# Between the projections of a recurrent branch: its element-wise work put between the projection tiles in another order, and the token turns of its hats put into the first inverse

## The chip, the cores and the metric

The kernel is one program on one core of a Trainium2 chip. The metric is the device time of one execution in microseconds (us). The engines run side by side and wait for one another by semaphores: TensorE (PE in the profile) multiplies matrices from SBUF into PSUM, VectorE (DVE), ScalarE (ACT) and GpSimd (POOL) work element by element, and SyncE (SP) issues the DMA transfers. Each engine takes its own instructions strictly in the order in which they were written.

## What is computed

Two transformer blocks follow each other on a sequence of 512 tokens of width 1024. The change touches the recurrent branch (`rwkv7_time_mix`) of the second block:

```python
def rwkv7_time_mix(p, shift_mu, w0, w2, a0, a2, g2, k_k, k_a, r_k, ln_x_w, ln_x_b):
    prev = jnp.pad(p, ((0, 0), (1, 0), (0, 0)))[:, :-1]
    p = p + (prev - p) * shift_mu
    r, k, v, cw, ca, cg = jnp.split(p, splits, axis=-1)
    w_log = -jax.nn.softplus(-(w0 + jnp.tanh(cw) @ w2)) - 0.5
    decay = jnp.exp(-jnp.exp(w_log.astype(jnp.float32)))
    a = jax.nn.sigmoid(a0 + ca @ a2)
    g = jax.nn.sigmoid(cg) @ g2
    kk = heads(k * k_k)
    kk = kk / jnp.maximum(jnp.sqrt(jnp.sum(kk * kk, axis=-1, keepdims=True)), 1e-12)
    k = k * (1.0 + (a - 1.0) * k_a)
    ...
    def step(state, inp):
        r_t, w_t, k_t, v_t, aa_t, bb_t = inp
        sa = jnp.einsum('bhij,bhj->bhi', state, aa_t)
        state = (state * w_t[:, :, None, :] + sa[..., None] * bb_t[:, :, None, :]
                 + v_t[..., None] * k_t[:, :, None, :])
        y = jnp.einsum('bhij,bhj->bhi', state, r_t)
        return state, y
```

`p` is the projection of the normalized input. The kernel runs the recurrence in chunks of 128 tokens: with cumulative decays the products of a chunk become matrix products, and each chunk needs the inverse of a triangular matrix.

## The kernel before

The projection `p` of the branch has 14 tiles of 128 features by 512 tokens: receptances r are tiles 0 to 3, keys 4 to 7, values 8 to 11, tile 12 holds the two low-rank inputs (decay in partitions 0 to 63, rate a in 64 to 127), and tile 13 the gate's. A tile is 24 matmuls of 128x512 on TensorE (`split_tile`, lines 611 to 613: 8 blocks of the contraction, three products of high and low parts each). Two tiles share one weight block. Each block is rounded by ScalarE (`split2_act`, L2525) and its remainder is taken by GpSimd (`splits2_pool`, L2537); TensorE waits for that before the first tile of a pair.

The functions of the stage, each written once for each engine and run in this order:

- `band_*`: the attention branch. Tile 0 of the recurrent branch is projected inside it.
- `shift_*`: the tiles 0 to 13 in that order, through two PSUM banks. VectorE scales a tile into a padded buffer `PADR` (L2827), takes the difference to the token before (L2829) and mixes (L2831); for keys it also multiplies by `k_k` (L2834). ScalarE squares (L2792), TensorE sums the squares by heads (L2767), and logarithm and exponential give the norm (L2796, L2801). After tile 13: the low-rank products (L2779, L2783), their tanh (L2809), and VectorE's scaling (L2847, L2849).
- `tiles_*`: for each of four tiles m of 128 features, VectorE's `decays` (the cumulative sum L2917 to the key product L2929 and the bonus product L2931) and `products` (L2936 to L2944), ScalarE's exponentials (L2886 to L2888), then TensorE's bonus sums (L2862) and the turn of three tiles into token order (hats `BH`, `KH`, and the values; L2873), copied by ScalarE (L2893).
- For each half of the heads: `units_*` (chunk products L2980, L2981, masked by VectorE L3034), `inverse2_*`, `state_*`.

`inverse2_pe` begins with eight steps of rows (`inv_rows_pe`, L1060: two matmuls of 128x256, one in the last) that alternate with fifteen elimination steps on VectorE (L1205, L1208) through two banks. Then come four `keep_busy` matmuls (L597), whose result nobody reads, and the first product of the assembly (L1075).

## Time and profile before

| | us |
|---|---|
| median of 3 runs | 2902.4 (2900.73 to 2904.36) |
| the profiled execution | 2909.93 |
| its span, first to last instruction | 2908.1 |
| first tile of `shift` on TensorE to the last: 2056.8 to 2133.1 | 76.3 |
| from there to the first chunk product (2179.3) | 46.2 |
| rows of the first inverse, first matmul to the first of the assembly (2194.9 to 2209.0) | 14.1 |

The profiled execution took 7.5 us more than the median of the unprofiled runs. Times within the trace are counted from the span's start. In a row of a timeline stand start, duration, engine, line, operation, output<-input, shapes and a count; in brackets, how long the engine had been idle and what ended it. A duration is that of the instruction with its pipeline: two that follow each other overlap a little, so the step from start to start is what a chain pays. An fp32 matmul leaves two records.

### The profile page before, as it was taken

The page shows a single profiled execution, that of the slowest core. Times are in us where ns is not written, and L with a number is a line of the kernel's source. Part 1 is how long each engine was busy: PE and PEld are TensorE (multiplying, and loading weights), DVE is VectorE, ACT ScalarE, POOL GpSimd, SP SyncE. Part 2 cuts the span into 40 slices and gives each one's busy share as a digit, 9 for nine tenths or more (in the row PEclk, how much of TensorE's full clock was granted, in tenths as well). Part 3 has the DMA queues.
Part 4 walks back from the last instruction along what each step waited for, and adds up shares of the span by engine and source line. Part 5 has one row for each costly group of instructions (what it writes and reads, how often), then busy time and mean ns, then how long its engine had stood idle before and what let it go on. Part 6 is the DMA issues. An engine that isn't in the chain of part 4 may idle for free.

```text
span 2908.1 us, 34074 instructions
## 1 busy us (share of the span) xinstructions
PE 2643.7 (91%) x14331; PEld 1725.7 (59%) x14331; DVE 1001.1 (34%) x1728; ACT 713.2 (25%) x1200; POOL 606.6 (21%) x185
## 2 busy tenths in 40 slices
PE   8999979879999998889888988898968899999998
PEld 7766767676658542333323323365757766788886
DVE  3267756753112311111011010134664522361331
ACT  3257633523112110010000100034231121321212
POOL 3301644623113000000000000041301122344442
PEclk9999969979999999999999999998978999999999
DMA  4302113104225799999999999951200033332231
GB/s 161 117 16 76 64 37 116 59 2 145 87 87 204 295 405 428 428 428 429 428 428 428 429 428 428 428 174 66 66 1 1 16 116 94 123 94 101 87 101 73
DMA packets 131044, 559.36 MB, mean 192 GB/s; under 512 B 7320, under 2 KB 88672, under 8 KB 103272
## 3 DMA queue, kind: packets, MB, share of 16 engines
q1 hardware_dynamic: 130056, 551.28, 48.1%
q0 software_dynamic: 864, 6.29, 0.6%
q8 instruction: 94, 1.54, 0.2%
q14 instruction: 30, 0.25, 0.0%
HBM read 547.01 MB, written 10.54 MB: 192 GB/s over the span
## 4 chain that ended last, share of the span: by engine, by line
PE 72%; DMA 13%; DVE 9%; ACT 4%; issue 2%; POOL 0%; DVEq 0%; SPq 0%; ACTq 0%; POOLq 0%
DMA S<-in_w_up 11%; PE PS L611 8%; PE PS L613 8%; PE PS L612 8%; PE PS L2215 7%; PE PS L2182 7%; PE PS L601 4%; PE PS L2165 2%; PE PS L3407 2%; PE PS L3409 2%; PE PS L3410 2%; PE PS L3245 2%; PE PS L2226 1%; DMA S<-in_w_down 1%; DVE PS L1205 1%
## 5 line engine op out<-in xcount | busy, mean ns | idle before, releaser
L2182 PE MATMUL PS<-S 128*64 128x512 f32 x2048 | 457.0, 596 | 72.2 <-DMA S<-in_w_up 68.0
L611 PE MATMUL PS<-r_block,r_block 128*128 128x512 f32 x1040 | 417.8, 402 | 4.2 <-POOL r_block L2537 2.3
L613 PE MATMUL PS<-r_block,r_block 128*128 128x512 f32 x1040 | 405.5, 390 | 0.0
L612 PE MATMUL PS<-r_block,r_block 128*128 128x512 f32 x1040 | 405.1, 390 | 0.0
L2537 POOL TENSOR_TENSOR r_block<-S,r_block 128x2048 fp32r<-128x2048 f32 x57 | 268.1, 4704 | 478.4 <-ACT r_block L2525 469.6
L2182 PEld LDWEIGHTS PS<-S 128*64 128x64 f32 x2048 | 140.9, 137 | 379.0 <-issue 247.4
L491 POOL TENSOR_TENSOR r_block<-S,r_block 128x2048 fp32r<-128x2048 f32 x40 | 183.3, 4582 | 551.7 <-ACT r_block L483 330.0
L2215 PE MATMUL PS<-S 128*64 128x512 f32 x1024 | 225.6, 597 | 6.6 <-DMA S<-in_w_down 3.3
L611 PEld LDWEIGHTS PS<-r_block,r_block 128*128 128x128 f32 x1040 | 195.5, 188 | 50.9 <-issue 9.0
L612 PEld LDWEIGHTS PS<-r_block,r_block 128*128 128x128 f32 x1040 | 195.6, 188 | 44.9 <-issue 5.8
L613 PEld LDWEIGHTS PS<-r_block,r_block 128*128 128x128 f32 x1040 | 195.3, 188 | 41.1
L2411 POOL TENSOR_TENSOR S<-S 128x1024 f32<-128x1024 f32 x4 | 9.5, 2407 | 976.9 <-DVE S L2399 976.9
L2525 ACT ACTIVATE r_block<-S 128x2048 fp32r<-128x2048 f32 x57 | 109.2, 1918 | 367.3 <-PE PS L613 196.2
L2374 DVE SCALAR_TENSOR_TENSOR S<-S,PS 128x512 f32<-128x512 f32 x32 | 22.0, 688 | 487.0 <-ACT S L2302 463.6
L2215 PEld LDWEIGHTS PS<-S 128*64 128x64 f32 x1024 | 75.8, 138 | 145.4 <-issue 140.6
L601 PE MATMUL PS<-S 128*128 128x512 f32 x256 | 110.5, 592 | 0.0
L2381 DVE TENSOR_TENSOR S<-S,PS 128x512 f32<-128x512 f32 x32 | 20.6, 684 | 256.4 <-PE PS L2182 256.4
L3407 PE MATMUL PS<-r_block,r_block 128*128 128x512 f32 x256 | 99.8, 390 | 1.6 <-DVE S L3457 1.6
L483 ACT ACTIVATE r_block<-S 128x2048 fp32r<-128x2048 f32 x40 | 76.4, 1909 | 99.2 <-DMA S<-in_w_in 68.4
L3409 PE MATMUL PS<-r_block,r_block 128*128 128x512 f32 x256 | 99.7, 389 | 0.0
L3410 PE MATMUL PS<-r_block,r_block 128*128 128x512 f32 x256 | 99.6, 389 | 0.0
L601 PEld LDWEIGHTS PS<-S 128*128 128x128 f32 x256 | 48.6, 190 | 59.6 <-issue 59.3
(487 smaller groups left out, 3768.7 us busy)
## 6 DMA issues: line engine op xcount, KB each, us to landing
S<-in_w_gate SPq DMA_DIRECT2D x64, 2048.0 KB, 17.9
S<-in_w_up SPq DMA_DIRECT2D x64, 2048.0 KB, 21.0
S<-in_w_down SPq DMA_DIRECT2D x64, 2048.0 KB, 25.6
S<-in_w_in SPq DMA_DIRECT2D x57, 1024.0 KB, 5.3
S<-in_w_up SPq DMA_DIRECT2D x16, 1024.0 KB, 5.5
S<-in_w_down SPq DMA_DIRECT2D x16, 1024.0 KB, 4.8
S<-decay_rows SPq DMA_DIRECT2D x8, 1024.0 KB, 7.0
S<-in_w_out SPq DMA_DIRECT2D x8, 1024.0 KB, 5.0
```

The lines of the kernel that those rows point to most:

```text
L491: pool.tensor_tensor(r32(w), w, rounded(WH[k % 2]), ALU.subtract).then_inc(sem("w_low"), 1)
L601: mm = pe.matmul(out, w[:, dc, off:off + P], src[:, dc, :], start=(dc == 0), stop=(dc == DC - 1))
L611: pe.matmul(out, wh, r32(HT[:, dc, :]), start=(dc == 0), stop=False)
L612: pe.matmul(out, wh, r32(low[:, dc, :]), start=False, stop=False)
L613: mm = pe.matmul(out, wl, r32(HT[:, dc, :]), start=False, stop=(dc == DC - 1))
L2182: mm = pe.matmul(PS[c * CAP:(c + 1) * CAP, 2 + 2 * m + g, :], XE[:, 2 * q + r, e * CAP:(e + 1) * CAP], w[:, r, 1024 * g + 512 * c:1024 * g ...
L2215: mm = pe.matmul(PS[c * CAP:(c + 1) * CAP, 6 + half, :], HE[e][:, f, :], w[:, f % 4, 512 * half:512 * half + 512], start=(f == 0), stop=(f ...
L2525: act.activation(r32(WH[k % 2]), slot2(name), ACT.Copy).then_inc(sem("w2_high"), 1)
L2537: pool.tensor_tensor(r32(w), w, rounded(WH[k % 2]), ALU.subtract).then_inc(sem("w2_low"), 1)
L3407: pe.matmul(PS[:, n, :], uh, r32(grid(wh.rearrange("p a b -> p (a b)"), 2)[:, f % 2, s]), start=first, stop=False)
L3409: pe.matmul(PS[:, n, :], uh, r32(wl[:, f % 2, s]), start=False, stop=False)
L3410: mm = pe.matmul(PS[:, n, :], ul, r32(grid(wh.rearrange("p a b -> p (a b)"), 2)[:, f % 2, s]), start=False, stop=last)
```

## The change

- The tiles come in the order 12, 13, keys 4 to 7, receptances 0 to 3, values 8 to 11 (`R_ORDER`), through four PSUM banks; i counts the place in that order below, t the tile.
- The shift is computed in another way: VectorE scales the tile into its frame, ScalarE writes mu times the tokens before into the tile's PSUM bank (511 columns), VectorE multiplies the frame's first column by 1-mu and then computes (1-mu) times the frame plus the bank.
- Low-rank products stand behind places 2 and 3, their tanh at 3 and 4, `decays` behind the scaling of places 3 to 6, head sums at place 6, norms at 7 to 9, `products` (with the bonus product) behind the scaling of places 9 to 12. Keys times `k_k`, and the square, are now computed by ScalarE. Norm logarithms and exponentials are computed in PSUM.
- The values are turned into token order behind places 12 and 13. The eight turns of the hats and the four bonus sums stand between the row steps of the first inverse, their copies on ScalarE after the inverse's corners, and TensorE waits for the last of them ahead of the `keep_busy`.
- `tiles_*` is gone. Low-rank weights load ahead of the branch's second weight block, the gate's weights ahead of the merge's first, and the third weight buffer of the branch lies in another place. LOW3, NORMF and SIG have other addresses.

The core of the diff (left out are addresses, semaphore tables, and removed lines that stand in the listing above):

```diff
+        R_ORDER = (12, 13, 4, 5, 6, 7, 0, 1, 2, 3, 8, 9, 10, 11)
...
+            load2(("r", j), cols2(a["w_in_2"], B2_R + P * R_ORDER[2 * j]), full, "r_proj", 2 * (j + 1))
...
+            third = B2 + 16384 if n < where2[("r", 0)] else M_X if n < where2[("m", 0, 0)] else B2 + 22528
...
+        KKN = [BH[:, m, :] for m in range(4)]
+        KSQ = [at(B2 + 15360 + 1024 * m, T) for m in range(4)]
+        CS = [TM[:, m, :] for m in range(4)]
+        KP = [TM[:, 4 + m, :] for m in range(4)]
...
+        def turn_pe(pe, n, src):
+            if n >= 2:
+                pe.wait_ge(*count("t_tok", n - 1))
+            for tc in range(TC):
+                mm = pe.transpose(PS[:, 6 + n % 2, block_of(tc)], src[:, block_of(tc)], ident)
+            mm.then_inc(sem("t_turned"), 1)
...
+        def hat_turn_pe(pe, j):
+            m, w = divmod(j, 2)
+            turn_pe(pe, 4 + j, (BH, KH)[w][:, m, :])
+
+        def tokens_act(act, n):
+            dst, m = (VT, n) if n < 4 else ((BT, KTK)[n % 2], (n - 4) // 2)
+            act.wait_ge(*count("t_turned", n + 1))
+            act.activation(dst[:, :, block_of(m)], grid(PS[:, 6 + n % 2, :], TC), ACT.Copy).then_inc(sem("t_tok"), 1)
+
...
+            def low_rank(m):
+                if m >= 2:
+                    pe.wait_ge(*count("r_gates", 2 * m - 3))
+                pe.matmul(PS[:, 4 + m % 2, :], W2[0:64, block_of(m)], FR[0:64, 12, :], start=True, stop=True)\
+                    .then_inc(sem("r_low"), 1)
+                if m >= 2:
+                    pe.wait_ge(*count("r_gates", 2 * m - 2))
+                pe.matmul(PS[:, 6 + m % 2, :], A2[64:128, block_of(m)], FR[64:128, 12, :], start=True, stop=True)\
+                    .then_inc(sem("r_low"), 1)
+
+            for i in range(1, 14):
+                if i % 2 == 0:
+                    await_split2(pe, ("r", i // 2))
+                if i >= 4:
+                    pe.wait_ge(*count("r_shift", i - 3))
+                split_tile(pe, PS[:, i % 4, :], parts2(("r", i // 2)), P * (i % 2), LOW3).then_inc(sem("r_proj"), 1)
+                if i == 2:
+                    pe.wait_ge(*count("lora_in", 32))
+                    pe.wait_ge(*count("r_lora", 1))
+                    low_rank(0)
+                    low_rank(1)
+                if i == 3:
+                    low_rank(2)
+                    low_rank(3)
+                if i == 6:
+                    pe.wait_ge(*count("r_gates", 8))
                     for m in range(4):
                         pe.wait_ge(*count("t_sq", m + 1))
                         pe.matmul(PS[:, 4 + m, :], const("heads2"), KSQ[m], start=True, stop=True).then_inc(sem("t_sum"), 1)
...
+                if i == 12:
+                    pe.wait_ge(*count("t_norm", 4))
+                    value_turn_pe(pe, 0)
+            for m in range(1, 4):
+                value_turn_pe(pe, m)
...
         def shift_act(act):
...
+            def gates(m):
+                for w, (dst, bias) in enumerate(((LW, s_w0h), (AG, s_a0h))):
+                    act.wait_ge(*count("r_low", 2 * m + w + 1))
+                    act.activation(dst[:, m, :], PS[:, 4 + 2 * w + m % 2, :], ACT.Tanh, bias=bias[:, m:m + 1], scale=0.5)\
+                        .then_inc(sem("r_gates"), 1)
+
+            def key_squares(m):
+                act.wait_ge(*count("r_shift", 3 + m))
+                act.activation(KKN[m], FR[:, 4 + m, :], ACT.Copy, scale=vec("k_k", m)).then_inc(sem("t_kk"), 1)
+                act.activation(KSQ[m], FR[:, 4 + m, :], ACT.Square, scale=vec("k_k", m)).then_inc(sem("t_sq"), 1)
+
+            def exps(m):
+                act.wait_ge(*count("t_cs", 2 * (m + 1)))
+                act.activation(KH[:, m, :], CS[m], ACT.Exp, scale=-1.0).then_inc(sem("t_exps"), 1)
+                act.activation(LW[:, m, :], LW[:, m, :], ACT.Exp).then_inc(sem("t_exps"), 1)
+
+            for i in range(14):
+                t = R_ORDER[i]
+                if i % 2 == 0 and i < 12:
+                    split2_act(act, ("r", i // 2 + 1))
+                act.wait_ge(*count("r_copied", i + 1))
+                act.activation(PS[:, i % 4, 1:T], frame(t)[:, 0:T - 1], ACT.Copy, scale=vec("mu", t)).then_inc(sem("r_prev"), 1)
+                if i == 1:
+                    act.wait_ge(*count("r_shift", 1))
+                    act.activation(FR[0:64, 12, :], FR[0:64, 12, :], ACT.Tanh).then_inc(sem("r_lora"), 1)
+                if i == 2:
+                    act.wait_ge(*count("r_shift", 2))
+                    act.activation(SIG, SIG, ACT.Tanh, scale=0.5).then_inc(sem("r_lora"), 1)
+                    act.wait_ge(*count("r_halves", 5))
+                if i == 3:
+                    gates(0)
+                    gates(1)
+                if i == 4:
+                    gates(2)
+                    gates(3)
+                if 3 <= i < 7:
+                    key_squares(i - 3)
+                if 5 <= i < 9:
+                    exps(i - 5)
+                if i == 8:
                     for m in range(4):
                         act.wait_ge(*count("t_max", m + 1))
...
+                        act.activation(PS[:, 4 + m, :], PS[:, 4 + m, :], ACT.Ln, scale=2.0 ** 30).then_inc(sem("t_ln"), 1)
                     for m in range(4):
                         act.wait_ge(*count("t_ln", m + 1))
...
+                        act.activation(PS[:, 4 + m, :], PS[:, 4 + m, :], ACT.Exp, scale=-0.5, bias=s_c30).then_inc(sem("t_rn"), 1)
+                    for m in range(4):
+                        act.activation(AR[m][:, :, 1, :], grid(CS[m], TC), ACT.Exp).then_inc(sem("t_exps"), 1)
+                if i == 9:
+                    act.wait_ge(*count("t_ends", 12))
+                    act.activation(e_mid, cmid, ACT.Exp).then_inc(sem("t_ends_exp"), 1)
+                    act.activation(e_end, cend, ACT.Exp).then_inc(sem("t_ends_exp"), 1)
+                    act.activation(e_rest, e_rest, ACT.Exp).then_inc(sem("t_ends_exp"), 1)
+                if i == 13:
+                    tokens_act(act, 0)
+            for n in range(1, 4):
+                tokens_act(act, n)
...
+            def decays(m):
+                C = CS[m]
+                Cg = grid(C, TC)
+                dve.wait_ge(*count("r_gates", 2 * m + 1))
...
+                dve.wait_ge(*count("r_gates", 2 * m + 2))
...
+                dve.wait_ge(*count("r_sig", 2 * m + 1))
...
+            def faded_keys(m):
+                dve.wait_ge(*count("r_sig", 2 * m + 2))
+                dve.tensor_scalar(KP[m], AG[:, m, :], vec("k_a", m), s_ka1[:, m:m + 1], ALU.mult, ALU.add).then_inc(sem("t_kp"), 1)
...
+                dve.tensor_tensor(KP[m], KP[m], FR[:, 4 + m, :], ALU.mult).then_inc(sem("t_kp"), 1)
...
+                dve.wait_ge(*count("t_norm", m + 1))
...
+                dve.tensor_tensor(KH[:, m, :], KP[m], KH[:, m, :], ALU.mult).then_inc(sem("t_hats"), 1)
+                dve.wait_ge(*count("t_exps", 8 + m + 1))
+                dve.wait_ge(*count("r_shift", 7 + m))
+                dve.tensor_tensor(AR[m][:, :, 1, :], AR[m][:, :, 1, :], grid(r, TC), ALU.mult).then_inc(sem("t_ar"), 1)
+                dve.wait_ge(*count("t_hats", 2 * m + 2))
+                dve.scalar_tensor_tensor(KP[m], r, vec("r_k", m), KP[m], ALU.mult, ALU.mult).then_inc(sem("t_bonus"), 1)
...
+            dve.tensor_scalar(s_mu1, vec("mu", 0, 14), -1.0, 1.0, ALU.mult, ALU.add).then_inc(sem("r_halves"), 1)
...
+            for i in range(14):
+                t = R_ORDER[i]
+                f = frame(t)
+                dve.wait_ge(*count("r_proj", i + 1))
+                dve.tensor_tensor(f, PS[:, i % 4, :], RSB, ALU.mult).then_inc(sem("r_copied"), 1)
+                if 3 <= i < 7:
+                    decays(i - 3)
+                if i == 7:
+                    for m in range(4):
+                        dve.wait_ge(*count("t_sum", m + 1))
+                        dve.tensor_scalar(PS[:, 4 + m, :], PS[:, 4 + m, :], 1e-24, None, ALU.max).then_inc(sem("t_max"), 1)
+                    faded_keys(0)
+                if i == 8:
+                    faded_keys(1)
+                    faded_keys(2)
+                    faded_keys(3)
+                if i == 9:
+                    for m in range(4):
+                        dve.wait_ge(*count("t_rn", m + 1))
+                        dve.tensor_tensor(KKN[m], KKN[m], PS[:, 4 + m, :], ALU.mult).then_inc(sem("t_norm"), 1)
+                if 9 <= i < 13:
+                    products(i - 9)
+                dve.wait_ge(*count("r_prev", i + 1))
+                dve.tensor_scalar(f[:, 0:1], f[:, 0:1], s_mu1[:, t:t + 1], None, ALU.mult)
+                dve.scalar_tensor_tensor(f[:, 1:T], f[:, 1:T], s_mu1[:, t:t + 1], PS[:, i % 4, 1:T], ALU.mult, ALU.add)\
+                    .then_inc(sem("r_shift"), 1)
+                if i == 6:
+                    dve.wait_ge(*count("r_lora", 2))
+                    dve.tensor_scalar(SIG, SIG, 0.5, 0.5, ALU.mult, ALU.add).then_inc(sem("r_sig"), 1)
 
...
-                pe.wait_ge(*count("t_tok", 12))
+                pe.wait_ge(*count("r_shift", 14))
+                pe.wait_ge(*count("t_ar", 8))
...
             for p in range(8):
                 inv_rows_pe(pe, w, n, sel, p)
+                if hf == 0:
+                    hat_turn_pe(pe, p)
+                    if p % 2:
+                        bonus_pe(pe, p // 2)
+            if hf == 0:
+                pe.wait_ge(*count("t_tok", 12))
...
+            if hf == 0:
+                for j in range(4, 12):
+                    tokens_act(act, j)
...
+            if hf == 0:
+                dve.wait_ge(*count("t_bonus_sum", 4))
+                dve.tensor_copy(bon, grid(PS[:, 5, 0:TC * H2], TC)).then_inc(sem("t_bon"), 1)
...
-                dve.wait_ge(*count("t_tok", 12))
+                dve.wait_ge(*count("t_tok", 4))
...
-                pool.wait_ge(*count("t_bon", 1))
-                pool.wait_ge(*count("t_tok", 12))
+                pool.wait_ge(*count("t_ar", 8))
+                pool.wait_ge(*count("t_bonus", 4))
...
+            pe.wait_ge(*count("t_bon", 1))
...
-                if n == where2[("r", 6)]:
-                    sp.wait_ge(*count("b_yat", 4))
+                if n == where2[("r", 1)]:
                     sp.dma_start(W2[0:64, :], a["w2_2"][0]).then_inc(sem("lora_in"), 16)
                     sp.dma_start(A2[64:128, :], a["a2_2"][0]).then_inc(sem("lora_in"), 16)
+                if n == where2[("r", 2)]:
+                    sp.wait_ge(*count("x2_kept", 16))
+                if n == where2[("m", 0, 0)]:
+                    sp.wait_ge(*count("r_proj", 14))
+                    sp.wait_ge(*count("low2_out", 32))
                     sp.dma_start(G2, a["g2_2"][0]).then_inc(sem("g2_in"), 16)
-                if n == where2[("m", 0, 0)]:
                     sp.wait_ge(*count("s_y", TC))
```

**Order, TensorE in the first inverse.** Before, the chunk products (L2981) are followed by all fifteen row matmuls, the `keep_busy` and the assembly:

```order
L2981 MATMUL PS<-S 128x256
L1060 MATMUL PS<-S 128x256 x15
L597 MATMUL PS<-S 128x256 x4
L1075 MATMUL PS<-S 64x32 x32
L597 MATMUL PS<-S 128x256
```

Now (line numbers are one higher; L2996 is the chunk product, L2770 a turn's four transposes, L2788 a bonus sum's four matmuls):

```order
L2996 MATMUL PS<-S 128x256
L1061 MATMUL PS<-S 128x256 x2
L2770 MATMUL PS<-S 128x128 x4
L1061 MATMUL PS<-S 128x256 x2
L2770 MATMUL PS<-S 128x128 x4
L2788 MATMUL PS<-S 128x2 x4
L1061 MATMUL PS<-S 128x256 x2
L2770 MATMUL PS<-S 128x128 x4
L1061 MATMUL PS<-S 128x256 x2
```

A turn, and behind every second one a bonus sum, now stands between any two row steps; four such pairs of turns in all.

**Order, VectorE at the last tiles of the projection.** Before, three instructions a tile:

```order
L2827 TENSOR_TENSOR S<-PS,S 128x512
L2829 TENSOR_TENSOR S<-S 128x512
L2831 SCALAR_TENSOR_TENSOR S<-S 128x512
L2841 TENSOR_TENSOR S<-S 128x512 x4
L2843 TENSOR_SCALAR S<-S 128x512
L2847 TENSOR_SCALAR S<-S 128x512
```

Now, one place (`products`, first column, mix; then the scaling of the next tile, L2943):

```order
L2962 TENSOR_SCALAR S<-S 128x1
L2963 SCALAR_TENSOR_TENSOR S<-S,PS 128x511
L2943 TENSOR_TENSOR S<-PS,S 128x512
L2916 TENSOR_TENSOR S<-S 128x4x128
L2919 TENSOR_TENSOR S<-S 128x512
L2921 TENSOR_TENSOR S<-S 128x512
L2923 TENSOR_TENSOR S<-S 128x512
L2926 TENSOR_TENSOR S<-S 128x4x128
L2928 SCALAR_TENSOR_TENSOR S<-S 128x512
L2962 TENSOR_SCALAR S<-S 128x1
L2963 SCALAR_TENSOR_TENSOR S<-S,PS 128x511
L2943 TENSOR_TENSOR S<-PS,S 128x512
```

Six instructions of `products` moved between the scaling of a tile and its mix, at four places.

**Order, ScalarE at place 8.** Before, the logarithms and the exponentials of the norm with the block splits between them and the tail's tanh behind:

```order
L2792 ACTIVATE S<-S 128x512 x2
L2525 ACTIVATE r_block_581<-S 128x2048
L2796 ACT_TABLE_LOAD
L2796 ACTIVATE S<-S 128x512 x4
L2801 ACT_TABLE_LOAD
L2801 ACTIVATE S<-S 128x512 x4
L2803 ACTIVATE S<-S 64x512
L2804 ACTIVATE S<-S 128x512
L2809 ACTIVATE S<-PS,S 128x512 x8
```

Now (L2527 is the split of a weight block, L2850 the tokens before, L2842 and L2843 exponentials of the decays, L2871 and L2874 the norms, L2876 the exponentials for `AR`):

```order
L2527 ACTIVATE r_block_643<-S 128x2048
L2850 ACTIVATE PS<-S 128x511
L2842 ACTIVATE S<-S 128x512
L2843 ACTIVATE S<-S 128x512
L2871 ACT_TABLE_LOAD
L2871 ACTIVATE PS<-PS 128x512 x4
L2874 ACT_TABLE_LOAD
L2874 ACTIVATE PS<-PS,S 128x512 x4
L2876 ACTIVATE S<-S 128x4x128 x4
L2850 ACTIVATE PS<-S 128x511
L2879 ACTIVATE S<-S 128x16
```

Twelve activations and both table loads stand in one row there, behind the split of one block and ahead of the next place's tokens and the next split.

## Rows read from the trace of the kernel before

**Rows 1.** Chain that ended last, from the last projection tile: start, us, what

```profile
2132.89 0.24 PE PS L613
...
2144.26 1.22 DVE S L2917
...
2175.39 0.70 DVE S L2944
...
2179.32 0.71 PE PS L2980 x4
```

**Rows 2.** Windows: stretch, length, busy (count) of PE, PEld, DVE, ACT, POOL, PEclk, DMA share, GB/s

```profile
2056.80:2133.00 76.20, 74.73 (x322) 59.91 (x320) 49.94 (x54) 21.84 (x21) 28.19 (x6) 1.00 0.20 62
2133.00:2179.30 46.30, 23.80 (x97) 17.47 (x97) 39.03 (x73) 19.58 (x36) 0.00 (x0) 0.67 0.00 0
...
2194.90:2201.00 6.10, 6.07 (x14) 4.54 (x15) 3.54 (x10) 0.00 (x0) 0.00 (x0) 0.50 0.01 3
2201.00:2206.10 5.10, 4.55 (x17) 2.73 (x16) 4.30 (x16) 0.00 (x0) 0.00 (x0) 0.99 0.01 2
```

**Rows 3.** VectorE's groups by line and shape, 2133 to 2180: busy us, mean ns

```profile
L2917 DVE TENSOR_TENSOR_SCAN S<-S 128x512 f32<-128x512 f32 x4 | 4.9, 1223 | 0.3
...
L2942 DVE TENSOR_TENSOR S<-S 128x512 f32<-128x512 f32 x4 | 2.8, 692 | 0.1
...
L2918 DVE TENSOR_SCALAR S<-S 128x512 f32<-128x512 f32 x4 | 2.1, 523 | 0.0
L2847 DVE TENSOR_SCALAR S<-S 128x512 f32<-128x512 f32 x4 | 1.7, 427 | 3.1 <-ACT S L2809 3.1
```

**Rows 4.** Timeline of ScalarE: a block split, a table load, four logarithms

```profile
2107.98 1.92 ACT L2525 ACTIVATE r_block<-S 128x2048 fp32r<-128x2048 f32 x1 [3.31 <-PE PS L613]
2109.91 1.28 ACT L2796 ACT_TABLE_LOAD   x1
2116.54 2.42 ACT L2796 ACTIVATE S<-S 128x512 f32<-128x512 f32 x4 [5.34 <-DVE S L2838]
```

**Rows 5.** Timelines of GpSimd and VectorE at three places, side by side

```profile
2088.21 4.63 POOL L2537 TENSOR_TENSOR r_block<-S,r_block 128x2048 fp32r<-128x2048 f32 x1 [6.26 <-ACT r_block L2525]
...
2088.40 4.72 DVE L2834 TENSOR_SCALAR S<-S 128x512 f32<-128x512 f32 x1
...
141.87 4.63 POOL L491 TENSOR_TENSOR r_block<-S,r_block 128x2048 fp32r<-128x2048 f32 x1 [6.79 <-ACT r_block L483]
...
145.56 0.95 DVE L907 TENSOR_TENSOR S<-S 128x1 f32<-128x1 f32 x1 [21.60 <-ACT S L786]
...
288.07 4.61 POOL L491 TENSOR_TENSOR r_block<-S,r_block 128x2048 fp32r<-128x2048 f32 x1 [7.82 <-ACT r_block L483]
...
288.92 0.68 DVE L1379 SCALAR_TENSOR_TENSOR S<-S,PS 128x512 f32<-128x512 f32 x1
```

**Rows 6.** Timeline of TensorE: head sums, and low-rank products behind an idle stretch

```profile
2113.16 3.59 PE L2767 MATMUL PS<-S 128*128 128x512 f32 x8
...
2136.17 1.10 PE L2779 MATMUL PS<-S 64*128 64x512 f32 x1 [3.05 <-ACT S L2803]
...
2140.09 0.59 PE L2779 MATMUL PS<-S 64*128 64x512 f32 x1
```

**Rows 7.** Timeline of TensorE in `tiles`: bonus sums and turns

```profile
2149.06 1.83 PE L2862 MATMUL PS<-S 128*128 128x2 f32 x8 [6.76 <-DVE S L2931]
...
2161.67 1.02 PE L2862 MATMUL PS<-S 128*128 128x2 f32 x8 [1.96 <-DVE S L2931]
...
2172.88 2.92 PE L2873 MATMUL PS<-S 128*128 128x128 f32 x12 [1.33 <-DVE S L2944]
...
2177.94 0.66 PE L2873 MATMUL PS<-S 128*128 128x128 f32 x4 [0.20 <-ACT S L2893]
```

**Rows 8.** Timeline of TensorE in the first inverse, from its first row matmul

```profile
2194.93 7.85 PE L1060 MATMUL PS<-S 128*128 128x256 f32 x20 [5.92 <-DVE S L1193]
...
2206.12 1.89 PE L597 MATMUL PS<-S 128*128 128x256 f32 x8
2208.99 1.20 PE L1075 MATMUL PS<-S 64*64 64x32 f32 x35 [0.98 <-DVE S L1218]
```

182 lines of the change are left out of this document (24 added, 158 removed), and 6 rows, old and new, of the table CHAINS.

## The prediction

> **What bounds the kernel now.** I read first the chain that ended last, around the recurrent branch [rows 1]. TensorE's last projection tile ends at 2133.1, VectorE's serial chain follows (it starts `decays` at 2144.26, ends `products` at 2175.39), and the next large TensorE work begins at 2179.32. Then the windows [rows 2]: up to 2133 TensorE is busy 74.73 of 76.20 us; in the 46.30 us behind, VectorE is busy 39.03 and TensorE 23.80, much of that at the half clock (0.67 on average). So this stage has two halves with different limits, and the second is all dependency: nothing of the merge or of the chunk products may start. In the first half VectorE is busy 49.94, but this contains waits inside instructions [rows 5]: GpSimd's split ran from 2088.21 for 4.63, and a VectorE instruction that began at 2088.40, and that takes 0.42 to 0.52 elsewhere [rows 3], took 4.72. An instruction with one operand in PSUM took its normal 0.68 beside such a split, at 288.92. The reader is to see that VectorE's room between tiles is less than its idle time.
>
> **The shift stage, up to tile place 6.** One tile costs TensorE (74.73 busy, less 3.4 of head sums) / 13 = 5.5 [rows 2]; I use 5.45. Place 1 starts at 2056.8 and place 2 ends at 2069.5, with the same wait for GpSimd's first split as before (1.5). New on TensorE behind it: four low-rank pairs. At the full clock a record takes 0.59 with its pipeline [rows 6], a step some 0.1 less; the two products of a pair run beside each other, two steps a pair, so 1.9 for the first two pairs. Place 3 ends at 2076.8. The third pair waits for a gate: VectorE's scaling 0.7, ScalarE's tokens before 0.6, one tanh 0.6: 2.0 idle. With the last two pairs place 4 starts at 2081.0, and three tiles end at 2097.3. Up to here TensorE pays 3.9 for the low-rank products and 2.2 for waits. Head sums cost 3.4 as before [rows 6], and 0.4 for the last square, since ScalarE does three 0.6 activations behind the scaling of place 6.
>
> **From there VectorE is the bound.** Terms from start to start: an fp32 SBUF instruction of 512 columns 0.62, or 0.72 where the next needs its result (0.69 in the row), a one-source one 0.35 to 0.5, a scan 1.2, a small copy about 0.1 [rows 3]. `decays` with its two scalings is 3.7, a faded key 1.2, `products` with the bonus 4.0, scaling plus first column plus mix 0.7 + 0.1 + 0.7 = 1.5. At place 5 VectorE comes late: ScalarE gets its tokens at 2093.4, does 2.2 of squares and exponentials, splits block 4 for 1.9 [rows 4], and GpSimd holds 2098.1 to 2102.7. VectorE's fourth `decays` waits that long. From 2102.7:
>
> - rest of place 6: 3.7 + 0.8 + 0.4 = 4.9, to 2107.6
> - place 7: 1.5, four maxima 2.5, one faded key 1.2 = 5.2, to 2112.8
> - place 8: 1.5, three faded keys 3.5, wait for GpSimd (split 5 runs to 2116.5) 3.1 = 8.1, to 2120.9
> - place 9: 1.5, four norms 2.5, `products` 4.0 = 8.0, to 2128.9
> - place 10: 1.5, `products` 4.0, wait for split 6 (to 2132.6) 3.1 = 8.6, to 2137.5
> - places 11 and 12: 5.5 each, to 2148.5
> - place 13: scaling 0.7, ScalarE 0.7, mix 0.8 = 2.2, to 2150.7
>
> TensorE for comparison: place 7 starts at 2101.1, place 11 ends at 2128.3. Place 12 needs split 6, and ScalarE is in its long row at place 8 from 2113.4: tokens 0.6, two exponentials 1.1, load 1.3, four logarithms 2.4, load 1.3, four exponentials 2.6, four more 2.4, then tokens and three small ones 1.0, to 2126.0 [rows 4]; then the split, 1.9, and GpSimd, 4.6: 2132.6. TensorE idles 4.3. Behind 3.05 idle its clock had fallen, and a low-rank record took 1.10 instead of 0.59 [rows 6]; I charge 1.7. Place 13 ends at 2146.0, 4.7 ahead of VectorE. So these waits on TensorE cost nothing beyond VectorE's sum; cut them and VectorE is still last. Two value turns with their copies remain, some 2.5 (0.97 each at the half clock, 2.92 / 3 [rows 7]): the chunk products start at 2153.5 instead of 2179.3. That is **25.8 us earlier**.
>
> **What is moved and costs nothing there.** SyncE's low-rank loads move ahead of the second block's; the new wait for `x2_kept` holds the third block's load, which the stage needs only 5 tiles later; the gate's weights are needed in the second half of the heads. ScalarE's extra 14 token writes (0.6 each, 8.4) fill idle time except the 0.7 at place 13. Any of them would cost its duration if TensorE were waiting for it. The mask's wait (`t_tok` 4), and GpSimd's select (1.9, now ahead of place 13's end) stay under the ten microseconds of chunk products.
>
> **The first inverse.** Here TensorE gets eight turns and four bonus sums. Before, its 30 row records plus gaps took 11.2 (2194.93 to 2206.1), led by VectorE's elimination, then `keep_busy` and assembly at 2208.99: 14.1 in all [rows 8]. The clock was half to about 2201 and full then [rows 2]; 14 records in 6.1 us give 0.42 to 0.44 each at half, and some 0.24 at full. At half clock: rows 1.7, turn 0.97, rows 1.7, turn 0.97, bonus 1.83 [rows 7] = 7.2. Then full: 22 row records 5.2, five turns 0.66 each 3.3, two bonus sums 1.02 each 2.0 = 10.5. Rows end after 17.7 instead of 11.2. Then the last turn and bonus 1.7 and `keep_busy` 1.9 [rows 8]: assembly after 21.3 instead of 14.1, **7.2 us more**. What covered them before is gone: TensorE, not VectorE, is now last at each row step. ScalarE's eight copies (0.6 each) follow each turn and are ready before the next but one. Bounds: all at full clock, rows end after 7.1 + 4.6 + 3.1 = 14.8 and the cost is 4.3; all at half, 30 x 0.43 + 7 x 0.97 + 3 x 1.83 = 25.2 and then 6.6, so 17.7. I take the value in between since the idle 5.92 ahead and the work that raised the clock are the same [rows 8].
>
> **Sum.** -25.8 + 7.2 = -18.6 us in the span of 2908.1. All behind the stage waits on it, so it shifts whole. The profiled execution lies 7.5 above the median of 2902.4; the difference carries over: **2883.8 us**.
>
> **A rule weighed.** Two things speak of the shared SBUF access. In [rows 5] a VectorE instruction of a single column with two SBUF inputs that began at 145.56 took 0.95, to the end of GpSimd's 4.63. No row shows a one-column instruction with one SBUF source beside a split. The Trainium skill, "SBUF — State Buffer", section "Who interferes with whom", says that copies and `tensor_scalar` can enter a two-port mode and then contend with GpSimd, the later one blocked for the whole of the earlier. By it the 14 new first-column instructions wait for a split too. Put into the walk above, the end moves by 0.2 us, since VectorE is blocked there by its large instructions anyway; without it the sum stands. By the same section whoever starts first holds the pair for a whole instruction, which is the third rival's mechanism in its weakest form.
>
> **Rivals.**
> - *Turns hidden, VectorE less blocked.* Were no wait for GpSimd paid, VectorE would end 3 to 4 earlier, where TensorE's own sum stands; with the turns at full clock, 4.3. Change -26 to -23: 2876 to 2880. For it: clock was up at 2201 with gaps in the work. Against: [rows 5]. Chance 0.15.
> - *Longer cross-engine chains.* Every hand-over between VectorE, ScalarE and TensorE costs some 0.05 in my walk; at 0.2, the end moves by 1.7; two more full locks of 4.6, or the half clock through the inverse (10.5 more), give -13 to -3: 2889 to 2899. Chance 0.22.
> - *Starved splits (slower).* VectorE issues strings of 4 us of SBUF instructions. If a string kept GpSimd out until its end ([rows 5] shows only VectorE as the one blocked), the six splits would start up to 4 later each, and TensorE's stall for each, with the clock lost (4 + 1.7) x 6 = 34, would exceed the 25.8 saved: with the 7.2, +15, 2918. It decides from about 3.1 us a split. Against: each place has two or three instructions with a PSUM operand that leave a gap. Chance 0.03.
> - *It doesn't do what it says*: if place 13's chain waited for something long on ScalarE, the tail of 46 would come back. The order shows nothing behind it. 0.01, within 0.2%.
>
> **How the numbers follow.** Forecast -23 to -13, 2879 to 2890: 0.59. With the two neighbours the range 2876 to 2892 holds some 8 in 10. A measurement of this kernel can tell about 0.2% (5.8 us) from no change: faster by more 0.92 (the forecast, the first rival and most of the second), within 0.05, slower 0.03.
>
> **What would show it.** In the profile after: first chunk product near 2153 and last projection tile near 2146; six GpSimd splits of 4.6 with VectorE instructions as long beside them; an idle stretch of 3 to 5 us on TensorE before place 12, released by GpSimd; from the first row matmul to the assembly 21 us instead of 14. Wrong would be: TensorE waiting for `r_shift` at earlier places (VectorE's terms too small), or a first inverse that has not grown.

## The result, and the profile after

The changed kernel took 2878.8 us (median of 4 runs, 2873.91 to 2883.0) and the kernel before 2901.68 (4 runs): ratio 0.9923, 95% interval 0.9906 to 0.994. That is 22.9 us less, where the forecast said 18.6. The profiled execution after took 2878.79 us, its span was 2877.0.

The two profiled spans differ by 31.1 us, more than the medians. Comparing when the same VectorE instruction starts in both traces shows which part is the change's. These are rows of the timeline of VectorE, first the last bias addition of the banded attention, which no edit touches, before and after; then the last group of the whole kernel, before and after:

```profile
2041.56 0.69 DVE L2725 SCALAR_TENSOR_TENSOR S<-PS,S 128x512 f32<-128x512 f32 x1 [1.05 <-PE PS L2630]
```

```profile
2032.97 0.69 DVE L2727 SCALAR_TENSOR_TENSOR S<-PS,S 128x512 f32<-128x512 f32 x1
```

```profile
2899.87 4.87 DVE L3359 SCALAR_TENSOR_TENSOR S<-S 128x1024 f32<-128x1024 f32 x4 [0.80 <-ACT S L3353]
```

```profile
2868.74 4.87 DVE L3387 SCALAR_TENSOR_TENSOR S<-S 128x1024 f32<-128x1024 f32 x4 [0.80 <-ACT S L3381]
```

So 8.6 us of the 31.1 had arisen in unchanged code ahead of the stage (the profiled execution before was 8.3 above the median of its four runs), and 22.5 are the change's. All stretches below are therefore distances between two instructions of one trace, not absolute times.

The chain that ended last, after, answers to [rows 1]: VectorE's last scaling, mix and the value turns now lead straight into the chunk products (L2995), at 2145.13 in the chain, where [rows 1] had 2179.32; the corners, the row matmuls (L1061), and between them turns and bonus sums (L2788), lead to the assembly (L1076):

```profile
2141.20 0.61 DVE S L2943
2141.84 0.69 ACT PS L2850
...
2143.19 1.94 PE PS L2770 x8
2145.13 1.16 PE PS L2995 x4
...
2146.90 9.67 DVE S L3061 x16
...
2161.13 2.05 PE PS L1061 x4
2163.18 0.85 PE PS L2770 x4
...
2168.92 0.87 PE PS L1061 x4
2169.78 0.44 PE PS L2770 x4
2170.22 0.79 PE PS L2788 x8
...
2177.57 1.89 PE PS L598 x8
2179.47 2.01 PE PS L1076 x64
```

The windows of after, with the columns of [rows 2]: the tiles; the 4.4 us before the value turns; turns, products and corners; the first inverse in two pieces; what follows it:

```profile
2047.90:2138.80 90.90, 84.17 (x349) 64.12 (x348) 66.24 (x115) 44.73 (x63) 27.60 (x6) 0.96 0.15 47
2138.80:2143.20 4.40, 0.56 (x6) 0.35 (x4) 3.64 (x8) 1.36 (x3) 1.89 (x1) 0.96 0.22 60
2143.20:2161.10 17.90, 12.15 (x72) 10.20 (x72) 10.51 (x19) 5.31 (x11) 4.46 (x1) 0.88 0.00 1
2161.10:2167.40 6.30, 6.27 (x25) 5.37 (x25) 3.08 (x8) 1.20 (x2) 0.04 (x1) 0.55 0.00 0
2167.40:2179.40 12.00, 12.00 (x80) 10.65 (x80) 7.20 (x25) 3.58 (x6) 1.80 (x1) 1.00 0.01 2
2179.40:2200.60 21.20, 19.98 (x447) 17.15 (x447) 6.70 (x12) 7.49 (x13) 0.95 (x1) 1.00 0.01 2
```

[Rows 2] had a second half of 46.3 us, in which VectorE was busy 39.03 and TensorE half of the time at a clock of 0.67. That half is gone: VectorE's work lies within the tiles, where it is now busy 66.24 of 90.9 us, and the clock there is 0.96.

From VectorE's first scaling (2058.88 before, 2049.60 after) to the first mask it is 121.68 us before and 97.30 after, -24.4. From the first row matmul to the assembly it is 14.06 before [rows 8] and 18.27 after, +4.2. Ahead of the first scaling 0.7 go, and behind the assembly another 1.5: the granted clock was 0.84 before in the 21 us behind it, and 1.00 after, and the first 25 us there are 2.0 shorter. Together -22.5, with 0.1 between mask and rows. This is that window of before:

```profile
2209.00:2230.00 21.00, 20.60 (x423) 17.10 (x424) 6.51 (x11) 7.04 (x12) 1.12 (x2) 0.84 0.01 2
```

### The profile page after: what moved, and what is told of

Its sections match the earlier page's. It is cut to its first block, busy times and chain, and to the rows that moved or that the text cites. A ratio compares the mean times of both kernels' runs of the same rounds, so it can differ in the third digit from the quotient of the medians.

```text
span 2877.0 us, 34074 instructions
## 1 busy us (share of the span) xinstructions
PE 2626.2 (91%) x14331; PEld 1711.4 (59%) x14331; DVE 982.3 (34%) x1724; ACT 723.9 (25%) x1218; POOL 605.7 (21%) x185
## 4 chain that ended last, share of the span: by engine, by line
PE 71%; DMA 13%; DVE 9%; ACT 4%; issue 2%; POOL 1%; DVEq 0%; SPq 0%; ACTq 0%; POOLq 0%
DMA S<-in_w_up 11%; PE PS L612 8%; PE PS L614 8%; PE PS L613 8%; PE PS L2216 7%; PE PS L2183 7%; PE PS L602 4%; PE PS L2166 2%; PE PS L3435 2%; PE PS L3437 2%; PE PS L3438 2%; PE PS L3273 2%; PE PS L2227 1%; DMA S<-in_w_down 1%; PE PS L633 1%
## 5 line engine op out<-in xcount | busy, mean ns | idle before, releaser
L2539 POOL TENSOR_TENSOR r_block<-S,r_block 128x2048 fp32r<-128x2048 f32 x55 | 257.9, 4690 | 484.5 <-ACT r_block L2527 475.8
L492 POOL TENSOR_TENSOR r_block<-S,r_block 128x2048 fp32r<-128x2048 f32 x40 | 183.3, 4582 | 551.0 <-ACT r_block L484 329.4
L612 PEld LDWEIGHTS PS<-r_block,r_block 128*128 128x128 f32 x1040 | 195.8, 188 | 56.3 <-issue 10.9
L2527 ACT ACTIVATE r_block<-S 128x2048 fp32r<-128x2048 f32 x57 | 109.2, 1918 | 337.6 <-PE PS L614 166.7
```

Of the source, the lines that this page charges most:

```text
L492: pool.tensor_tensor(r32(w), w, rounded(WH[k % 2]), ALU.subtract).then_inc(sem("w_low"), 1)
L612: pe.matmul(out, wh, r32(HT[:, dc, :]), start=(dc == 0), stop=False)
L2527: act.activation(r32(WH[k % 2]), slot2(name), ACT.Copy).then_inc(sem("w2_high"), 1)
L2539: pool.tensor_tensor(r32(w), w, rounded(WH[k % 2]), ALU.subtract).then_inc(sem("w2_low"), 1)
```

## The experiments

Whole times of one kernel scatter by 10 to 20 us, stretches of equal code by 0.1 where the clock is the same. So the table gives both. Every kernel is the changed one with one edit, unless said otherwise. P0, P4 and P9 are VectorE's scalings of places 0, 4 and 9, M the first mask, R the first row matmul, A the assembly; P0-M is the time from P0 to M, and so on; us. The ratio is that of runs taken together on one chip; the medians of different chips are compared with less confidence.

| kernel | P0-M | P4-M | P9-P10 | M-R | R-A | median | ratio to before, 95% |
|---|---|---|---|---|---|---|---|
| changed | 97.3 | 66.1 | 7.8 | 14.2 | 18.3 | 2878.8 | 0.9923 (0.9906 to 0.994) |
| changed, again | 97.3 | 65.7 | 7.8 | 14.5 | 17.4 | 2880.2 | 0.9927 (0.9909 to 0.9946) |
| turns_ahead | 109.8 | 79.8 | 7.8 | 14.8 | 14.1 | 2885.9 | 0.9956 (0.9935 to 0.9978) |
| turns_units | 97.5 | 66.2 | 7.8 | 18.3 | 14.1 | 2880.9 | 0.9946 (0.9925 to 0.9966) |
| turns_idle | 98.3 | 65.1 | 7.8 | 14.2 | 14.1 | 2875.0 | 0.9889 (0.987 to 0.9907) |
| lowrank_later | 96.6 | - | 7.8 | 14.3 | 17.2 | 2879.5 | 0.9927 (0.9904 to 0.995) |
| short_splits | 94.8 | 63.2 | 9.7 | 14.2 | 17.1 | 2875.1 | 0.9911 (0.9879 to 0.9943) |
| products_last | 108.2 | 78.2 | 5.4 | 14.3 | 17.2 | 2887.4 | 0.9938 (0.9918 to 0.9959) |
| split6_early | 99.1 | 67.8 | 12.1 | 14.4 | 17.3 | 2881.0 | 0.9915 (0.9898 to 0.9931) |
| no_max | 97.7 | 66.4 | 7.8 | 14.2 | 18.3 | 2876.4 | 0.9909 (0.9886 to 0.9933) |
| split6_ln | 95.5 | 64.1 | 9.4 | 14.6 | 14.1 | 2872.7 | 0.9908 (0.9884 to 0.9931) |
| rebalanced | 95.6 | - | 13.3 | 14.2 | 14.1 | 2869.4 | 0.9899 (0.9879 to 0.9918) |
| rebalanced2 | 95.2 | - | 11.4 | 14.2 | 14.1 | 2874.2 | 0.9909 (0.9894 to 0.9924) |

The step from place 3 to place 4, with the low-rank pairs, took 10.7 to 13.9 us in the ten kernels that have the same code there, depending on TensorE's clock behind its wait of 2.17 us. These are its windows (length, TensorE busy, clock, DMA) from the first of these products on, in the changed kernel and in products_last, where the clock stayed up behind the same wait:

```profile
2071.03:2075.03 4.00, 4.00 (x9) 0.57 0.64 224
```

```profile
2074.91:2078.91 4.00, 4.00 (x13) 1.00 0.65 225
```

In turns_idle it came back only within place 4. That is why P4-M stands beside P0-M. The changed kernel run again confirms the result:

> The changed kernel once more, unaltered, on the same chip as the two others, as the yardstick for both: 0.992 of the kernel before; its stretches as in its first profile: place 4 scaling to first mask 66.1, first mask to first row matmul 14.2, first row matmul to assembly 17 to 18.3. If the 22.9 us of the first comparison were partly chance, the ratio would come out above 0.994.

### Where the turns cost least

**turns_ahead.**

```diff
 # shift_pe, behind the value turns
+... (waits for the hats and the bonus products)
+for p in range(8):
+    hat_turn_pe(pe, p)
+    if p % 2: bonus_pe(pe, p // 2)
 # inverse2_pe
-if hf == 0:
-    hat_turn_pe(pe, p)
-    if p % 2: bonus_pe(pe, p // 2)
 # ScalarE's eight copies move with them (left out)
```

> The changed kernel with its eight hat turns and four bonus sums taken out of the first inverse and put on TensorE right behind the value turns, ahead of the chunk products. My theory (in the inverse they cost 4.2 us, since TensorE then is last at each row step; ahead of the products nothing hides them but 1 us or so): the stretch from the first row matmul to the assembly falls back from 18.3 to about 14, and the first mask comes 6 to 8 us later (eight turns of 0.66 and four bonus sums of 0.8 at the full clock, 8.5, of which the first turns may begin while TensorE idles before 2143), so 2 to 4 us slower than the changed kernel: about 2881 to 2883. Rival 1 (the turns in the inverse cost nothing themselves, the 4.2 us there are the half clock that any stretch behind an idle one has): the inverse stays at 17 to 18, and the kernel is 6 to 8 us slower, 2886. Rival 2 (what costs in the inverse is the whole 8.5): the time stays, 2879.

The inverse fell to 14.1, as before the change, but the first mask came 12.5 us later, not 6 to 8. TensorE's timeline:

```profile
2140.05 3.80 PE L2770 MATMUL PS<-S 128*128 128x128 f32 x16 [3.93 <-ACT S L2784]
2143.64 1.70 PE L2788 MATMUL PS<-S 128*128 128x2 f32 x8
2145.21 1.95 PE L2770 MATMUL PS<-S 128*128 128x128 f32 x8
2146.95 1.71 PE L2788 MATMUL PS<-S 128*128 128x2 f32 x8
```

Behind the 3.93 idle a pair of turns took 1.74 from start to start and a bonus sum 1.56 (2145.21 to 2146.95 to 2148.51), twice the 0.88 and 0.79 that they take in the changed kernel's chain: all 15 us up to the chunk products passed at a granted clock of 0.50. From place 4 the mask is 13.7 later. My theory was right on where they cost more and had the size too small, by the clock; the time came out at rival 1's 2886, whose mechanism the inverse of 14.1 refutes. Against the plain place ahead of the products, hat turns and bonus sums in the inverse saved 13.7 + 0.6 - 4.2, some 10 us by the stretches and 7 by the medians.

**turns_units** puts a hat turn behind every second chunk product and the bonus sums behind them all.

```diff
 # units_pe, in the loop over the 16 products
+if n in (3, 5, 7, 8, 9, 11, 13, 15):
+    hat_turn_pe(pe, ...)
 # behind the products of m == 1
+for k in range(4): bonus_pe(pe, k)
 # left out: a wait for the bonus products; the turns leave the inverse,
 # and ScalarE's copies stand ahead of its corners
```

> The changed kernel with its eight hat turns put between the chunk products of the first half (one after every second product) and the four bonus sums behind the products, ahead of the first row matmul, where TensorE waited 5.8 us. My theory (turns cost only where TensorE is last; between the products VectorE's 16 masks of 0.61 set the pace and TensorE is busy 8.35 of 14 us): first mask and first row matmul stay within 1 us of their distance from the stage's start, the stretch from first row matmul to assembly falls from 18.3 to 14 or below, since TensorE is busy right before it and its clock is up: 4 to 6 us faster than the changed kernel, 2873 to 2875. Rival 1 (the half clock comes whatever TensorE did before): the inverse falls to 14 only, 2875. Rival 2 (the turns wait for ScalarE's copies and delay the chunk products and so the masks by 4 us or more): no gain, 2879.

Rival 2 held in size, not in cause. The inverse lost its 4.2, and M-R grew by 4.1. ScalarE's copies did not set the pace: the last ended at 2158.84, and ScalarE's first corner began at 2158.97, 0.12 behind VectorE's copy L1189, as in the changed kernel (0.11). Two chunk products with a turn need 1.65 of TensorE at the full clock where two masks need 1.29 of VectorE, which now waited for TensorE:

```profile
2152.57 0.66 PE L2770 MATMUL PS<-S 128*128 128x128 f32 x4
2153.16 0.71 PE L2995 MATMUL PS<-S 64*128 64x256 f32 x4
2153.70 0.60 PE L2996 MATMUL PS<-S 64*128 64x256 f32 x4
2154.23 0.66 PE L2770 MATMUL PS<-S 128*128 128x128 f32 x4
...
2158.04 3.63 PE L2788 MATMUL PS<-S 128*128 128x2 f32 x32
2163.50 2.04 PE L1061 MATMUL PS<-S 128*128 128x256 f32 x4 [1.83 <-DVE S L1194]
```

```profile
2155.98 1.29 DVE L3063 TENSOR_TENSOR S<-PS,S 128x512 f32<-128x512 f32 x2 [0.37 <-PE PS L2996]
```

The four bonus sums, 3.63, lay in an idle stretch and cost nothing. And even with TensorE at work until 2161.7 the first rows ran at half the clock (2.04 for four records, 2.05 in the changed kernel), but the inverse came to the same 14.1 as before the change.

**turns_idle** uses what the two had shown.

```diff
 # shift_pe, behind tile place 13
+value_turn_pe(pe, 1)
+for j in range(5): hat_turn_pe(pe, j)
 # shift_act, ahead of the write for place 13
+for n in range(5): tokens_act(act, n)
 # inverse2_pe: the four bonus sums ahead of the rows;
 # only hat turns 5 to 7 stay, behind row pairs 4 to 6
 # left out: waits, and the order of the copies
```

> The changed kernel with five hat turns put behind tile place 13, where TensorE idled 3.84 us (2139.3 to 2143.2) until ScalarE had copied the first value turn (that copy now comes ahead of ScalarE's write for place 13), the four bonus sums behind the chunk products, where TensorE idled 5.8 us (in the run with the turns between the products they took 3.63 there and delayed nothing), and three hat turns left in the last rows of the inverse. My theory (an instruction of TensorE costs nothing only where TensorE idles in the present order, and eight turns between the products cost 3.9 since there VectorE waited for TensorE at every second mask): place 0 scaling to first mask stays at 97 to 98 us, first mask to first row matmul at 14.2, first row matmul to assembly falls from 18.3 to 14 to 15.5. Sum 3 to 4 us less than the changed kernel, 2875. Rival 1 (what the turns cost follows them wherever they stand: 12.5 ahead, 3.9 between the products, 4.2 in the inverse): no gain. Rival 2 (ScalarE, whose five copies now precede its write for place 13, delays the last mix by their 3.3): the first mask 2 to 3 us later, gain 1.

As the theory had it: P4-M 65.1 (1.1 less), M-R 14.2, R-A 14.1, in all 5.3 less than the changed kernel; the medians, from two comparisons, say 3.8, and the two ratios, 0.9889 and 0.9923, have intervals that just touch, so that the gain rests on the stretches. Rival 1 falls: what a turn costs depends on the place.

### Who is last in the tiles

**lowrank_later** (`if i == 3` to `if i == 4` ahead of `low_rank(2)`, `low_rank(3)`).

> The changed kernel with the last two of the four low-rank pairs behind tile place 4 in place of 3. In the changed kernel TensorE waits 2.17 us for a tanh gate there, and its eight products then run at the half clock for 3.95 us. My theory: at place 4 the gates are long done, no wait and no half clock, so place 4 starts about 6 us earlier and place 5 about 4 us earlier (two pairs at the full clock take about 2); VectorE, which from place 6 on has no idle time, starts its gapless stretch 4 us earlier, and the chunk products start 3 to 4 us earlier: 2875. Rival 1 (the stage is bound later by GpSimd's split 6 and the ScalarE row before it, which follow VectorE's places): the same 3 to 4 us. Rival 2 (VectorE is the bound over the whole stage from place 3, so that an earlier tile 4 changes nothing): first mask as in the changed kernel, 2879. Rival 3 (GpSimd's locks fall on other instructions and give the gain back): 0 to 1 us.

Rival 3. Place 4 came 5.2 us earlier as expected (26.0 instead of 31.2 behind P0), but only 0.7 of it reached the first mask. At place 6 TensorE waited 2.3 for ScalarE's square, which now stood behind a block split, and VectorE was caught by GpSimd more fully:

```profile
2093.73 4.73 POOL L2539 TENSOR_TENSOR r_block<-S,r_block 128x2048 fp32r<-128x2048 f32 x1 [9.76 <-ACT r_block L2527]
```

```profile
2093.99 4.75 DVE L2895 TENSOR_SCALAR S<-S 128x512 f32<-128x512 f32 x1
```

**short_splits** (GpSimd's remainder of blocks 4, 5 and 6 replaced by a memset of the same tile).

```diff
+if name in (("r", 4), ("r", 5), ("r", 6)):
+    pool.memset(rounded(w), 0.0)
+    continue
 pool.tensor_tensor(r32(w), w, rounded(WH[k % 2]), ALU.subtract)
```

> The changed kernel with GpSimd's remainder of the recurrent blocks 4, 5 and 6 left out: a memset of the same tile stands in its place, so the low weight part of six tiles is zero and the output loses precision there. In the changed kernel the three remainders took 4.6 us each and three VectorE instructions beside them took 4.39, 3.23 and 3.65 in place of 0.43, 0.54 and 0.69, 9.6 us more; TensorE waited 2.9 us for the last. A memset of this size on GpSimd took 1.80, and VectorE instructions with SBUF operands beside it were not longer (0.76, 0.71). My theory (VectorE is the bound from place 6 on, its lost time counts until TensorE's own sum takes over: tile place 13 would end 2.9 + 1.7 earlier, and VectorE's scaling, mix and the value turns follow it): first mask 5 to 7 us earlier than in the changed kernel, 2872 to 2874. Rival 1 (TensorE and not VectorE is the bound): only the 2.9 us wait and its clock go, 3 to 4.6 us. Rival 2 (full slope, VectorE alone): 9.6 us, 2869. Rival 3 (the long instructions are no loss, the waits only moved): 0.

It gave 2.9 us (P4-M), less than my theory, near the lower end of rival 1. These are VectorE's waits in it:

```profile
DVE S L2946 <- PE PS L614: 4.1, 4, 2.8
DVE S L2961 <- ACT PS L2877: 1.7, 1, 1.7
```

Of the first lock, of 3.9 us, nothing was to be had: place 7 came 9.36 behind place 6 in both kernels, since TensorE needs that long for head sums and tile. Of the second 2.2 came off the step from place 8 to 9 (7.62 to 5.43, which is TensorE's tile), and 1.8 went back into the next step, where VectorE waited for ScalarE's exponentials. Only the third came off whole, 8.40 to 5.42. So the prediction's statement that VectorE is the bound from place 6 on, with all its locks on the path, falls: three engines lie within 3 us of each other.

**no_max** takes 2.5 us of work off VectorE at place 7 (`bias=s_tiny` in the logarithm, no `ALU.max`).

> The changed kernel without VectorE's four maxima of 2.48 us in all at tile place 7: the lower bound of the head sums is added inside ScalarE's logarithm instead, which no longer waits for VectorE. Theory after the short splits (taking 9.6 us of locks off VectorE moved the first mask by only 2.5 us, since VectorE then waited 2.8 for TensorE's place 7 and 1.7 for ScalarE's norms row): VectorE, TensorE and ScalarE's row lie within 3 us of each other at places 7 to 9, so 2.5 us off VectorE alone gives 1.5 to 2.5, and ScalarE's row starts 1 to 2 us earlier, which takes its wait away too: first mask 1.5 to 2.5 us earlier, 2877. Rival 1 (slope one, VectorE alone is the bound): 2.5, and with the earlier row more is to be had in the short splits only. Rival 2 (TensorE sets the pace at places 7 to 9): 0 to 0.5.

Rival 2: P4-M 66.4, no gain at all, although the median happens to be 2.4 lower. Place 7 was TensorE's (5.44 from scaling to scaling, 0.39 of it idle on VectorE), and place 8 began when it did before.

**products_last** moves the four `products(m)` behind the loop over the places.

> The changed kernel with the four calls of the products taken out from between tile places 9 to 12 and put behind the mix of place 13, so that only the decays, maxima, faded keys and norms are left between the tiles. Theory (in the changed kernel VectorE sets the pace at these places, but TensorE is close below it: its own place 13 ended at 2138.7 with 2.9 of waiting, VectorE's last scaling began at 2141.1): the last scaling moves 1 to 2.5 us ahead, and 24 instructions of 0.69 or 16.3 us stand behind the mix, with the value turns beside them: first mask 10 to 13 us later than in the changed kernel, 2889 to 2892. So about half of the 24.4 us that this stage got shorter is due to the products between the tiles. Rival (TensorE's half clock and the locks matter more than the place of VectorE's work): under 6 us, 2885.

P4-M grew by 12.1 and P0-M by 10.9, 10 to 13 expected. So putting the products between the tiles is worth about half of the 24.4 us. How the other half divides is not shown: no run moves decays, squares, maxima, keys or norms back, and the parts need not add up, since turns_ahead alone made P0-M 12.5 longer.

**split6_early.**

```diff
 # shift_act, place 8, behind the exponentials of the norms
+split2_act(act, ("r", 6))
 for m in range(4):
     act.activation(AR[m][:, :, 1, :], ..., ACT.Exp)
```

> The changed kernel with ScalarE's high part of the sixth recurrent block taken from ahead of tile place 10 and put into its long row at place 8, between the four exponentials of the norms and the four of the receptance side. GpSimd then begins the split about 3 us earlier, and TensorE's wait of 2.9 us ahead of place 12 and the half clock behind it (24 products, about 1.7) should be gone. Theory (VectorE is the last at places 9 to 13, with TensorE's place 13 ending 2.4 us before VectorE's last scaling begins): the wait goes, VectorE's lock of 3 us only moves to another instruction, and place 0 scaling to first mask stays at 97.3, 2879. Rival 1 (TensorE is the bound): 3 to 4.6 us less, 2875. Rival 2 (the exponentials behind it, 1.9 later, are then late for VectorE's products of place 9): 1 to 2 us more, 2880 to 2881.

TensorE's wait ahead of place 12 went, and P4-M grew by 1.7, which is rival 2's size but not its cause (no exponential was late). As expected the waits of TensorE there cost nothing beyond VectorE's, but the lock did not only move. It hit a string of products in full, 4.3 in place of 3.0; P9-P10 is 12.1 instead of 7.8, P10-P11 then 5.4 instead of 8.4. These are GpSimd and VectorE:

```profile
2122.07 5.02 POOL L2539 TENSOR_TENSOR r_block<-S,r_block 128x2048 fp32r<-128x2048 f32 x1 [7.92 <-ACT r_block L2527]
```

```profile
2122.65 4.99 DVE L2922 TENSOR_TENSOR S<-S 128x512 f32<-128x512 f32 x1
```

**split6_ln** is turns_idle with the same line between the logarithms and the exponentials, so that GpSimd works while VectorE does the norms, whose operand is in PSUM.

> The kernel with the turns in TensorE's idle stretches (turns_idle) and, beside that, ScalarE's high part of block 6 put between the four logarithms and the four exponentials of the norms. In split6_early GpSimd's split began just as VectorE's products did, and the step from place 9 to place 10 took 12.1 us instead of 7.8. Theory (the lock costs VectorE nothing while it runs the four norms, whose operand lies in PSUM): GpSimd's split now falls on the norms; they start 1.9 later, behind the exponentials, but the 3.0 us of the lock at place 10 go, and TensorE's wait of 2.9 us ahead of place 12 goes: place 4 scaling to first mask 65.1 in turns_idle, here 63.5 to 64.5. Rival 1 (the norms are blocked too): 67 or more. Rival 2 (the price of a split on VectorE is the same wherever it falls): 65 to 66.

P4-M 64.1, as forecast. GpSimd and VectorE, side by side:

```profile
2106.86 4.62 POOL L2539 TENSOR_TENSOR r_block<-S,r_block 128x2048 fp32r<-128x2048 f32 x1 [4.18 <-ACT r_block L2527]
```

```profile
2108.79 2.48 DVE L2968 TENSOR_TENSOR S<-S,PS 128x512 f32<-128x512 f32 x4 [1.36 <-ACT PS L2886]
2111.19 0.84 DVE L2926 TENSOR_TENSOR S<-S 128x512 f32<-128x512 f32 x1
```

Four norms took 2.48 under the split (2.47 without one); the lock cost 0.15 instead of 3.0, and half of that gain went into the wait of 1.36 for the later exponentials.

### All together

**rebalanced** joins turns_idle, lowrank_later and no_max, moves ScalarE's split behind its squares at place 6, and spreads the faded keys.

```diff
 # shift_dve: faded keys 0, 1 at place 7; 2 at place 8; 3 at place 9
 # shift_act
+if i == 6: split2_act(act, ("r", 4))   # behind key_squares(3)
+if i == 7: split2_act(act, ("r", 5))   # behind exps(2), then Ln x4
 # place 8: Exp x4 of the norms, exps(3)
+split2_act(act, ("r", 6))
```

> Several edits together: turns_idle; the low-rank pairs 2 and 3 behind place 4; ScalarE's high parts of blocks 4 and 5 behind its squares at place 6 and behind its exponentials at place 7, that of block 6 behind the exponentials of the norms; the logarithms at place 7 without VectorE's maxima; and two faded keys at place 7, one at 8 and one at 9. Theory (VectorE, TensorE and ScalarE are within 1 to 3 us of each other at each place, so only edits to all three together pay): TensorE's wait of 2.2 and its half clock at place 4 go (4 us, which lowrank_later gave back since TensorE waited 2.3 for ScalarE's squares at place 6 and VectorE 4.3 for a split), places 7 and 8 run at TensorE's 5.4 each (13.1 together in the changed kernel): place 0 scaling to first mask 89 to 92 us (97.3 in the changed kernel), the inverse at 14.1, so 9 to 12 us less than the changed kernel: 2867 to 2870. Rival (what one engine gains the next lock takes, as in lowrank_later): 94 to 96, and 2872.

By the stretches it is 1.7 below the changed kernel up to the first mask and 4.2 in the inverse, not the 9 to 12 hoped for. Place 9 came 61.7 behind P0 instead of 64.5, but then the sixth split met the products: 4.99 for one, P9-P10 13.3. The rival's 94 to 96 us hold for this stretch. Its median, 2869.4 on the chip on which the changed kernel gave 2880.2, is the lowest; the two intervals overlap.

**rebalanced2** moves that one line ahead of the exponentials.

> The rebalanced kernel with one line moved: ScalarE's high part of block 6 ahead of the four exponentials of the norms instead of behind them. In rebalanced, GpSimd's split began at 2113.24, just as VectorE had finished the norms, and one product took 4.99 instead of 0.69: the step from place 9 to 10 took 13.3 us. In split6_ln the same split fell on the norms, none of them was longer (2.48 for four, 2.47 without a split), and the step took 9.4. Theory (the lock costs VectorE only what it meets with all operands in SBUF, so its place decides): norms about 2112.7 to 2115.1 on the clock of rebalanced, split over at 2115.4, so the products are 2 us earlier: place 9 to place 10 in 11 to 11.5, place 0 scaling to first mask 93.5 to 94 (95.6 in rebalanced), 2867 by the stretches. Rival (each split costs VectorE its 3 to 4 us wherever it falls): 95.6, no change.

P9-P10 fell to 11.4, as forecast, but from the last scaling to the first mask it was 5.8 instead of 4.4: TensorE now idled longer ahead of the turns, and turns and first products ran at a clock of 0.71 instead of 1.00. So only 0.4 was left of 2. Four kernels with the turns in idle stretches have medians of 2869.4 to 2875.0, all below the 2878.8 and 2880.2 of the changed one; which of the four is best can't be told from these runs.

## Why the prediction was right

**The tiles.** The walk gave 25.8 less from the first matmul of place 1 to the first chunk product, and that is what was measured: 122.5 before (2056.80 to 2179.32), 96.7 after (2048.31 to 2145.06). The 24.4 above are the same gain between VectorE's marks: 0.8 of it lies ahead of the first scaling, and 0.6 went again behind the first chunk products, which ran at the half clock (1.23 for four records instead of 0.71). Place by place, from scaling to scaling, places 7 to 12 were forecast at 5.2, 8.1, 8.0, 8.6, 5.5 and 5.5 and measured at 5.44, 7.62, 7.81, 8.40, 5.42 and 5.42, the last place at 2.3 instead of 2.2. The rows of the timeline of VectorE, answering to [rows 5], show the locks at places 6, 8 and 10:

```profile
2092.26 4.39 DVE L2892 TENSOR_SCALAR S<-S 128x512 f32<-128x512 f32 x1
...
2107.05 3.23 DVE L2909 TENSOR_SCALAR S<-S 128x512 f32<-128x512 f32 x1
...
2122.48 3.65 DVE L2916 TENSOR_TENSOR S<-S 128x512 f32<-128x512 f32 x1
```

The first term that was off is the third low-rank pair. The wait was 2.17 (2.0 forecast), but the four products of the last two pairs (eight records) ran at the half clock, 3.95, where I had reckoned 2: my 1.10 row of [rows 6] had stood there for it. In turns_ahead and products_last, where the clock stayed at 1.00 behind the same wait, the step to place 4 was 1.2 shorter, so some 2.8 for the same products. A part of the sizes fit for a reason I had not seen: places 7, 11 and 12 are as long for TensorE (5.43) as for VectorE (5.42), so it made no difference to the sum which of them is "the bound". It does make one to what further cuts are worth, as no_max and short_splits show.

That the sum came out to a tenth is luck. Counted from the first matmul of place 1, which the walk has at 2056.8 and the trace of after at 2048.31, place 4 began 2.5 us later than forecast and place 7's scaling 1.9 later; places 7 to 12 took 0.8 less than forecast, and the value turns 1.6 behind the last mix instead of 2.8.

**TensorE's stall ahead of place 12.** Forecast 4.3, released by GpSimd; measured 2.9, released by GpSimd, with eight matmuls at half the clock behind it (0.63 instead of 0.39):

```profile
2125.64 0.69 PE L612 MATMUL PS<-r_block,r_block 128*128 128x512 f32 x1 [2.91 <-POOL r_block L2539]
```

It was shorter because TensorE's place 11 ended 2.9 later than in the walk and the split only 1.5 later. "Costs nothing beyond VectorE's sum" holds: split6_early took the wait away and gained nothing.

**The first inverse.** 7.2 more were forecast between bounds of 4.3 and 17.7; 4.2 were measured, just below the lower bound; in the second run and four others with the same inverse it was 3.0 to 3.3, in no_max 4.2. The mechanism stands: with all turns out, or all but three, R-A is 14.07 or 14.08 in six kernels, and 14.06 before. But TensorE was not last "at each row step": VectorE waited for it at four of the later steps, three of them behind a turn and a bonus sum, for 0.85, 1.17, 0.65 and 1.15, together 3.8 of the 4.2. What failed is the size of the term. At the full clock turns and bonus sums were priced at the 0.66 and 1.02 of their records [rows 7], but a record reaches past the start of the next, and the chain pays 0.44 and 0.79: 6 x 0.22 + 3 x 0.23 = 2.0 too much. And the half clock ended after 6.3 us, not 7.2. That is 2.9 of the 3.0. The same prices made the lower bound too high.

**What the sum left out.** It had nothing for the 1.5 us behind the assembly, where the clock was 0.84 before and is 1.00 after. The turns in the inverse are not its cause: all twelve other profiles have 1.00 there too, turns_ahead and turns_units among them, which have no turn in the inverse. This is turns_ahead's window behind its assembly (length, TensorE busy, clock, DMA):

```profile
2186.31:2207.31 21.00, 19.78 (x445) 1.00 0.01 2
```

The kernel before has one profile only, so the cause stays open, chance included.

With 0.7 + 24.4 + 0.1 - 4.2 + 1.5 the sum is 22.5. The range of 2876 to 2892 held the time, at its lower side, and the neighbour "turns hidden, VectorE less blocked" (-26 to -23, 2876 to 2880), to which I gave 0.15, holds the time, while my own interval of 2879 to 2890 just misses it. That rival was nearly right in the turns and wrong in the locks: VectorE still paid them.

**The rivals.** Longer cross-engine chains: no, from place 7 on the steps agree to 0.5. Starved splits: no. GpSimd's six splits took 4.56 to 4.67, in a string of VectorE instructions or not; the longest of any run was 5.02, in split6_early. It began at 2122.07, while a VectorE instruction ran, and the next of VectorE began at 2122.65, so it seems to have waited some 0.4 for one instruction. The fourth rival, that the kernel doesn't do what it says: no, the tail of 46 us is gone. Two signs came out smaller than said: the idle stretch was 2.9, not 3 to 5, and the inverse 18.3, not 21.

**The rule weighed.** The Trainium skill, "SBUF — State Buffer", section "Who interferes with whom", says that a `tensor_scalar` can enter a two-port mode, when its operands meet certain conditions, and then contends with GpSimd. I had read it so that the one-column instruction would wait too. No row of before showed one beside a split. After does, for a split that began at 2050.91 and one at 2120.92, 4.58 and 4.67 long:

```profile
2051.59 0.21 DVE L2962 TENSOR_SCALAR S<-S 128x1 f32<-128x1 f32 x1 [1.30 <-ACT PS L2850]
...
2121.11 0.21 DVE L2962 TENSOR_SCALAR S<-S 128x1 f32<-128x1 f32 x1
```

It took 0.21, as without a split, here and wherever it met a GpSimd split in the twelve profiles without the memset (20 times), while the `tensor_scalar` of 512 columns took 4.39. The measurement decides: read that way, the rule does not hold for this shape; for the 512 columns it agrees.

## What to carry to other kernels

Moving a serial chain of VectorE into the room between matmul tiles pays until all engines have the same length per tile. Walk it place by place, with the locks: from place 7 on each step here held to 0.5 us, but the exact total owed something to errors that cancelled. From there on taking work off one engine gives little (2.5 us of maxima: 0; 9.6 of locks: 2.9), and a GpSimd split should be timed to fall on VectorE instructions that read PSUM. Small TensorE work belongs where TensorE idles anyway, right behind its last work; in the chain of an engine that is barely slower it costs much of its own time, and behind an idle stretch, at the half clock, it cost twice its time in turns_ahead.

## What was not expected of the hardware

- The same eight turns and four bonus sums cost 12.5 to 13.7 us ahead of the chunk products, 4.1 between them, 4.2 in the inverse, and nothing that the stretches show with the bonus sums and five turns in idle stretches and three turns in the last rows.
- In turns_ahead the granted clock stayed at 0.50 (1.2 GHz) for 15.3 us in which TensorE was busy for 15.15 with turns and bonus sums; in turns_units it was down behind 3.63 us of bonus sums and 1.83 idle, where the first four row records took 2.04. But behind the same idle 2.17 ahead of the third low-rank pair the clock fell in some kernels and stayed at 1.00 in others.
- A one-column `tensor_scalar` passed beside a GpSimd `tensor_tensor` (0.21), a 512-column one did not (4.39). A GpSimd memset of 1.8 held up a `tensor_scalar` of 512 columns in short_splits (1.62 instead of 0.43, to the memset's end), but not, it seems, a `tensor_tensor` of 512 columns, all in SBUF, that began 1.2 into the third one (0.68). I had expected it to hold up neither.
